# The start byte of the weight slots' halves within a 512-byte line

## What is computed

```python
h = rmsnorm(x, ln1_g[l]); proj = h @ w_in[l]
x = x + mix @ w_out[l]
x = x + jnp.square(jax.nn.relu(h2 @ w_up[l])) @ w_down[l]
# second block, per layer
x = x + 0.5 * _swiglu(_rms_norm(x, ffn1_norm[l]), ffn1_wi[l], ffn1_wo[l])
c = _split_cols(u @ w_in[l] + b_in[l])
x = x + merged @ w_out[l]
x = x + 0.5 * _swiglu(_rms_norm(x, ffn2_norm[l]), ffn2_wi[l], ffn2_wo[l])
```

## Time and profile before

| | |
|---|---|
| median of the runs | 2405.95 us |
| span of the profiled execution | 2406.4 us |
| PE busy | 2379.8 us (99% of the span) |
| PE weight loads (beside the matmuls) | 1924.6 us (80%) |
| POOL busy | 1316.2 us (55%) |
| DVE busy | 1209.2 us (50%) |
| ACT busy | 965.8 us (40%) |
| transfers from and to HBM | 213.40 MB, 89 GB/s over the span |

### The profile page before, as it was taken

One profiled execution on the slowest core, in us unless ns is written; L12 is line 12 of the kernel. 1 busy time (PEld: TensorE's weight loads), 2 busy tenths in 40 slices (PEclk: granted clock), 3 DMA queues, 4 the chain that ended last, 5 costly groups with the idle time before them and its releaser, 6 DMA issues.

```text
span 2406.4 us, 29717 instructions
## 1 busy us (share of the span) xinstructions
PE 2379.8 (99%) x11108; PEld 1924.6 (80%) x11108; DVE 1209.2 (50%) x1961; ACT 965.8 (40%) x1513; POOL 1316.2 (55%) x1589
## 2 busy tenths in 40 slices
PE   8999999999999999999999999999999999999999
PEld 8777778888888888777787888888887777788887
DVE  5997765423224432379625743333325785266331
ACT  4554444322223223566524432332336764344321
POOL 5763246656556655366244765555554562466554
PEclk9999999999999999999999999999999999999999
DMA  5321123333333333222122333333332221223333
GB/s 166 109 71 53 47 77 97 96 97 97 97 97 110 97 97 103 71 72 69 54 87 79 97 97 97 96 97 97 97 98 67 72 78 53 88 87 98 96 97 96
DMA packets 59758, 213.40 MB, mean 89 GB/s; under 512 B 6624, under 2 KB 6752, under 8 KB 59488
## 3 DMA queue, kind: packets, MB, share of 16 engines
q1 hardware_dynamic: 59472, 211.38, 29.2%
q10 hardware_dynamic: 144, 0.14, 0.0%
HBM read 209.39 MB, written 2.10 MB: 88 GB/s over the span
## 4 chain that ended last, share of the span: by engine, by line
PE 91%; DVE 6%; issue 1%; ACT 1%; DMA 0%; POOL 0%; SPq 0%; DVEq 0%; ACTq 0%
PE banks L721 89%; DVE t L1203 1%; DVE t L1211 1%; DVE t L1213 1%; DVE t L1488 1%; DVE t L1204 1%; DVE t L1197 1%; DVE t L1219 0%; PE banks L841 0%; PE banks L995 0%; DVE t L1222 0%; ACT t L1679 0%; DMA t<-in_w 0%; PE banks L875 0%; POOL t L1992 0%
## 5 line engine op out<-in xcount | busy, mean ns | idle before, releaser
L721 PE MATMUL banks<-t,t 128*128 128x512 f32 (+4 forms) x10788 | 2351.7, 387 | 17.2 <-ACT t L1699 5.9
L721 PEld LDWEIGHTS banks<-t,t 128*128 128x128 f32 (+2 forms) x10788 | 1889.5, 188 | 452.2 <-issue 64.3
L1992 POOL TENSOR_TENSOR t<-t,t 128x256 fp32r<-128x256 f32 x1544 | 1258.9, 846 | 1049.9 <-ACT t L1679 1041.5
L1679 ACT ACTIVATE t<-t 128x1024 fp32r<-128x1024 f32 x385 | 408.2, 1060 | 1078.8 <-issue 605.5
L1197 DVE TENSOR_TENSOR t<-banks,t 128x512 f32<-128x512 f32 x121 | 83.1, 687 | 169.8 <-PE banks L721 169.2
L1378 DVE TENSOR_TENSOR t<-banks,t 128x512 f32<-128x512 f32 x44 | 30.4, 690 | 184.5 <-PE banks L721 184.3
L1346 DVE SCALAR_TENSOR_TENSOR t<-banks,t 128x512 f32<-128x512 f32 x32 | 22.1, 691 | 155.4 <-PE banks L721 155.4
L1080 DVE SCALAR_TENSOR_TENSOR t<-t,t,t 128x512 fp32r<-128x512 f32 x64 | 52.0, 817 | 58.1 <-ACT t L1699 58.1
L1323 DVE TENSOR_TENSOR t<-t,t 128x512 fp32r<-128x512 f32 x68 | 70.5, 1036 | 2.3
L1352 DVE TENSOR_TENSOR t<-banks,t 128x512 f32<-128x512 f32 x24 | 16.6, 691 | 106.0 <-PE banks L721 106.0
L1699 ACT ACTIVATE t<-t,t 128x512 fp32r<-128x512 f32 x64 | 45.6, 715 | 55.7 <-DVE t L1346 49.1
(11 more groups left out here) (182 smaller groups left out, 1304.7 us busy)
## 6 DMA issues: line engine op xcount, KB each, us to landing
t<-in_w SPq DMA_DIRECT2D x386, 512.0 KB, 3.5
t<-in_xT SPq DMA_DIRECT2D x8, 256.0 KB, 5.7
out<-t SPq DMA_DIRECT2D x8, 256.0 KB, 4.5
t<-in_dmask SPq DMA_DIRECT2D x1, 1536.0 KB, 7.7
t<-in_vbias SPq DMA_DIRECT2D x2, 384.0 KB, 4.1
t<-in_c SPq DMA_DIRECT2D x1, 576.0 KB, 8.6
t<-in_w SPq DMA_DIRECT2D x2, 256.0 KB, 3.9
t<-in_pos SPq DMA_DIRECT2D x2, 256.0 KB, 4.1
```

The source lines that it names most:

```text
L721: return pe.matmul(o, l, r, start=start, stop=stop, skip_group_check=True)
L1679: a.activation(whl[u % 2][:, 0:1024], wraw[u % 3][:, :], ACT.Copy).then_inc(*w_high.next(u))
L1992: p.tensor_tensor(hl[:, 1024:2048][:, c], wraw[u % 3][:, c], as_f32(hl[:, c]), ALU.subtract).then_inc(*w_low.next((u, q)))
```

## The change

The two weight slots are moved by 384 bytes, from byte 128 of a line to byte 0 of the next, and 128 bytes are added behind them, so that everything behind is 512 bytes farther on and stands at its old byte of a line.

```diff
         wraw = [take(1024) for _ in range(3)]
+        top[0] += 384
         whl = [take(2048, F32R) for _ in range(2)]
+        top[0] += 128
         tab = take(2 * S)
```

## The result

The changed kernel takes 2448.86 us (median of 4 runs, 2447.9 to 2449.62), the kernel before 2406.89 us beside it. The ratio is 1.0173 with a 95% interval of 1.016 to 1.0185: **slower by 42 us**. The profiled execution spans 2446.0 us, 39.6 more than before.

What follows compares the result with a forecast made beforehand. PE's matmuls were taken to bound the kernel, number times distance. The 2406.4 us span plus 0 for ACT and POOL, loads and stream, with the runs' median 0.45 us lower, gave 2406 us; range 2312 to 2450.

Steps and rivals of the forecast that it cites:

- rival B: Dense stream: stationary and moving operands at different bytes keep it unsettled, 393 for 389 ns, 35 us, 2441 us; chance 0.28.
- The bound: PE, 91% of the chain: time is the number of matmuls times their start-to-start distance, 226.67 ns.
- ACT, POOL and the length of the loads: Weight split on ACT and POOL, covered by matmuls: 0 to +1 us; PE's 188 ns loads, unchanged: 0.
- The stream: PE's matmuls beside the loads: distance stays at the even 226.67 ns, 0 us, ends -117 and +79 us.
- a jolt rather than a price: Matmuls on mask_r operands at byte 192: 398, then 393 ns, taken as a passing disturbance of the stream.
- Rival A: Dense stream: byte 128, putting blocks across two lines, costs the fixed part; gain 88 us, 2318 us; chance 0.30, whole or part.
- the fixed part: Each matmul's distance beyond one column a cycle: about 13.3 ns whatever its width, 117 us over 8784 matmuls.
- The rule of the two read ports: PE's independent ports for moving operand and weight loads: by it a load's address cannot reach the stream, change worth 0.
- The wide products: 624 matmuls whose moving operands go to byte 0: taken as 0, between 8 us saved and 6 us lost.

Runs made afterwards that it cites:

- e7: Kernel before with weight slot 0 moved to byte 448, slot 1 (laid behind the hidden values' region) to 64, hidden values to 480; 2449.16 us (one run).
- e10: Kernel before, tiles unmoved, with second and third matmul of each dense block using 64 of the 128 stationary columns; 2490.89 us (one run).
- e12: Kernel before, tiles unmoved, with 23 of the 24 matmuls of a dense eight-block product using 64 of 128 stationary columns; 2533.07 us (one run).

## Why the prediction was right, and where it was not

**The number** was right by a narrow margin and partly by luck. The forecast of 2406 us missed by 43 us. What held the 2449 was the upper end of the range, 2450, put a little above rival B's 2441; a move of the slots to byte 192 or 160 measured 2454.64 and 2457.77 us, outside it.

**The bound** held: the time is the number of matmuls times their distance, and 95% of the loss stands in four pieces of the chain that hold nothing but PE's matmuls. The reading of 226.67 ns and of its evenness was the right row to start from.

**ACT, POOL and the length of the loads** were costed at 0 and are: 739 and 1062 ns, and 188.

**The stream** is the step that failed. The forecast took 0 between -117 and +79 us, where the four pieces show +37.7, on two arguments. The first was that the even distance held for both halves, both slots and all eight blocks. That was no evidence: all of these lie at multiples of 512 bytes from each other, hence at one distance modulo 256, and I had noted myself that the trace has only one such value. The place with 256 moving columns was no better: it has the same distance, and there the changed kernel came out quicker. The second was that the stationary operand at byte 192 gave "a jolt rather than a price". With the slots at that byte the price was 233.25 - 226.67 = 6.6 ns a matmul and 46 us in all. Two matmuls are too few to see a pattern in; their mean of 395.5 was already the right size, since the slots at 192 show 393 to 398.

**Rival B** is what happened, for nearly the reason given: a different byte for stationary and moving operand, in the dense stream, on PE alone. Its term of 4 ns was too small; it measured 232.44 - 226.67 = 5.8 ns. The 393 ns of the earlier trace rows was the median of a stretch that already ended in the even state. So it gave 2441 us for a measured 2449, inside the range. Its wording "no longer settles" is only half right, as the stream settles into another pattern.

**Rival A** was given a chance of 0.30 and fell: all tiles at byte 0 gave 2407 us. The bf16 figure of 215.7 ns on the Trainium skill's page "TensorE: Matmul & The Clock Gate", section "Wait — 56ns, not 53.3ns?", was no guide to what an fp32r stream could reach by alignment: no distance that was run came below 226.6 ns at 512 columns. Its premise that an address can give back some of the fixed part isn't empty, though: at 256 columns 14 ns were left over the columns' own time, and the 276 ns records of e7 leave 276 - 162 - 106.7, about 7.

**The rule of the two read ports.** The Trainium skill's page "SBUF — State Buffer", section "Who interferes with whom", has PE wait for nobody. The runs differ: with the same instructions and clock, the start byte of the operands alone changes the stream from 226.67 to between 229 and 234 ns. The measurement decides. That the delay arises at a read port is not shown.

**The wide products** were priced between -8 and +6 us. They went both ways: the records with 256 columns got 2 ns shorter, those with 384 about 3 ns longer, which is under 1 us in all for each (estimates, 192 x 2 and 96 x 3 ns). The 288 with 512 columns were not told apart from the dense ones. The piece with 542 matmuls, which holds 256-column ones too, still grew by 1.39 us.

**Left open:** what in the reads makes the pattern (the runs show that the cost repeats every 256 bytes, that it depends on the size of the load, and that at 512 columns an even stream was sure only where all operands agreed), why the products with 256 moving columns were quicker at unequal bytes, and what the fixed 13.3 ns of an fp32r matmul consist of.

## What to carry to other kernels

Where a stream of fp32r matmuls with 512 moving columns bounds a kernel, give stationary and moving operands, high and low halves alike, the same start byte modulo 256; bytes 0 and 128 did equally well, and an allocator's odd padding ahead of one of them costs up to 3% of the stream. Don't carry the rule to another width untried: at 256 moving columns equal bytes were the slowest. Read the minimum and maximum of a quiet stretch beside its mean: 388 to 390 is the good state, 390 to 404 or an even 396 is not. Evidence that holds for many addresses counts for one if all of them are equal modulo the step that matters.

## What the runs showed of the hardware

- The distance between fp32r matmuls of 128 x 128 by 512 depends on (stationary byte - moving byte) modulo 256: 226.7 ns at 0, 229 at 192, 232 to 234 at the other multiples of 32. It follows fixed patterns, such as 229 and 238 ns in turn.
- With 256 moving columns it is the other way round: records of 283 ns at equal bytes, 281 and 279 with the slots moved by 384 and by 64 bytes, and 276 in one stretch of e7.
- At distances of 16 and -16 bytes the same code ran even (389 ns records) in one stretch and uneven (387 to 398) in another of the same execution.
- Stationary operands of 64 columns in place of 128 made the stream slower, 229.4 (e10) and 230 ns (e12) against 226.7, though PEld was busy for 39.77 and 35.61 us of 60 against 49.73.
